# Forget sums of the attention added to the scores by a second product, and one expert matrix loaded at another place

## The reference, cut to what matters

```python
log_f = jax.nn.log_sigmoid(f_logit + b_forget)
cum = jnp.transpose(jnp.cumsum(log_f, axis=1), (0, 2, 1))
...
s = einsum('bqhd,bkhd->bhqk', qblk, kp) * scale
s = s + (cum[:, :, qs:qe, None] - cum[:, :, None, :qe])
s = jnp.where(s_pos <= t_pos, s, -inf)
p = softmax(s)
```

## Time and profile before

| what | value |
|---|---|
| time, median of three runs | 2497.79 us |
| the three runs | 2493.71, 2497.79, 2498.93 us |
| the profiled execution's own time | 2491.84 us |
| its span | 2490.1 us |
| PE busy | 1983.1 us, 80% |
| DVE, ACT, POOL busy | 1100.6, 421.6, 977.0 us |
| mean DMA rate over the span | 345 GB/s |

### The profile page before, as it was taken

One profiled execution on the slowest core, in us unless ns is written; L12 is line 12 of the kernel. 1 busy time (PEld: TensorE's weight loads), 2 busy tenths in 40 slices (PEclk: granted clock), 3 DMA queues, 4 the chain that ended last, 5 costly groups with the idle time before them and its releaser, 6 DMA issues.

```text
span 2490.1 us, 21117 instructions
## 1 busy us (share of the span) xinstructions
PE 1983.1 (80%) x7462; PEld 1022.2 (41%) x7462; DVE 1100.6 (44%) x2634; ACT 421.6 (17%) x1107; POOL 977.0 (39%) x1059
## 2 busy tenths in 40 slices
PE   8837997779988779989777777789999975566555
PEld 4523552235444225435322222248887732222221
DVE  6579638952457954455975444421012130000001
ACT  2312411201311111311111111101023110000000
POOL 0036757774556775546777777600000000000000
PEclk9868999999999999999999999999989988887887
DMA  6279999999999999999999999966543589999996
GB/s 221 93 262 338 409 402 407 409 409 399 402 357 406 409 409 402 399 372 342 409 409 409 409 409 409 410 208 166 151 101 121 191 342 426 428 426 427 427 427 266
DMA packets 228318, 860.19 MB, mean 345 GB/s; under 512 B 26080, under 2 KB 26592, under 8 KB 216432
## 3 DMA queue, kind: packets, MB, share of 16 engines
q0 software_dynamic: 147456, 536.94, 54.8%
q1 hardware_dynamic: 77488, 312.04, 33.1%
q10 hardware_dynamic: 3264, 9.80, 1.0%
HBM read 857.64 MB, written 1.05 MB: 345 GB/s over the span
## 4 chain that ended last, share of the span: by engine, by line
PE 37%; DMA 28%; DVE 18%; POOL 8%; issue 5%; ACT 2%; SPq 1%; DVEq 0%; ACTq 0%
PE psum L1840 13%; DMA rows<-in_peer_v,idx 8%; PE psum L2031 8%; DVE rows L1051 7%; PE psum L1832 6%; DMA rows<-in_w_e_gate 5%; POOL rows L691 4%; DMA rows<-in_w_e_down 4%; POOL rows L703 4%; DMA rows<-in_peer_u,idx 4%; DMA rows<-in_w_e_up 3%; PE psum L2234 3%; DMA rows<-in_gla_w_in 2%; PE psum L2257 1%; DVE work L934 1%
## 5 line engine op out<-in xcount | busy, mean ns | idle before, releaser
L2031 PE MATMUL psum<-rows,diag 128*128 128x512 f32 x2024 | 983.7, 625 | 264.6 <-ACT diag L1559 136.7
L1051 DVE CUSTOM_DVE_ANT_0 rows<-rows,psum 128x1024 f32<-128x1024 f32 x512 | 614.8, 1220 | 294.0 <-DMA rows<-in_peer_u,idx 283.2
L2031 PEld LDWEIGHTS psum<-rows,diag 128*128 128x128 f32 x2024 | 370.1, 195 | 832.1 <-issue 508.2
L691 POOL DMA_INDIRECT rows<-in_peer_u,idx x512 | 489.5, 956 | 378.2 <-DVEq L728 144.7
L703 POOL DMA_INDIRECT rows<-in_peer_v,idx x512 | 483.7, 945 | 272.6 <-PE psum L2031 148.6
L1840 PE MATMUL psum<-work,rows 128*128 128x256 f32 (+1 forms) x1664 | 287.9, 335 | 0.7 <-ACT work L1378 0.7
L1840 PEld LDWEIGHTS psum<-work,rows 128*128 128x128 f32 x1664 | 260.4, 193 | 31.0 <-issue 5.8
L1559 ACT ACTIVATE diag<-ident,wgt 128x128 f32<-128x128 f32 x506 | 166.0, 389 | 332.1 <-DVE wgt L1059 332.1
L2234 PE MATMUL psum<-rows,work 128*32 128x512 f32 x896 | 136.2, 693 | 106.0 <-DMA kept<-in_w_e_up 46.4
L1321 DVE TENSOR_TENSOR work<-kept,psum 128x512 f32<-128x512 f32 x8 | 8.2, 1030 | 423.2 <-PE psum L2234 423.2
L1378 ACT ACTIVATE work<-psum 128x512 f32<-128x512 f32 (+4 forms) x158 | 81.2, 532 | 547.7 <-PE psum L1840 194.9
(11 more groups left out here) (309 smaller groups left out, 1342.9 us busy)
## 6 DMA issues: line engine op xcount, KB each, us to landing
rows<-in_w_e_up SPq DMA_DIRECT2D x28, 2048.0 KB, 20.1
rows<-in_w_e_gate SPq DMA_DIRECT2D x25, 2048.0 KB, 20.5
rows<-in_w_e_down SPq DMA_DIRECT2D x24, 2048.0 KB, 20.9
rows<-in_w_in SPq DMA_DIRECT2D x32, 1024.0 KB, 9.6
rows<-in_gla_w_in SPq DMA_DIRECT2D x24, 1024.0 KB, 18.4
rows<-in_peer_w_query SPq DMA_DIRECT2D x16, 1024.0 KB, 9.2
rows<-in_peer_u,idx POOLq DMA_INDIRECT x512, 11.7
rows<-in_peer_v,idx POOLq DMA_INDIRECT x512, 12.1
```

The costliest lines, as they stand in the source:

```text
L691: pool.indirect_dma_start(out=u_rows[:, n % RU, :], out_offset=None, in_=a["peer_u"][g // 2], in_offset=bass.IndirectOffsetOnAxis(ap=idx[: ...
L1051: V_.tensor_tensor_reduce(out=u, in0=u, in1=tokens, scale=1.0, scalar=0.0, op0=ALU.mult, op1=ALU.add, accum_out=hid[:, r:r + 1]).then_inc( ...
L2031: last = mm(psum[:, 6 + c, :], diag[:, at % DIAGS, :], v_rows[:, n % RV, c * BANK:(c + 1) * BANK], start=r == 0, stop=summed(n + 1) == sum ...
```

## The change

The `fb` jobs, their copies, the bias tiles and DVE's two sums go. Each score product is left open and followed by a second one into the same columns of the bank, whose weight is the head's column of the identity repeated 128 times, and whose moving operand is the 16-row tile of running sums. So that they enter with the right sign, the scan subtracts. DVE adds the causal mask where it added the bias. PE waits for the copy of `k3` before the first scores. The first gate matrix (round 0, expert 0, place 0) is issued by ACT ahead of the mixer's first copy, once all value rows have been used.

```diff
-                + [f"fb{i}" for i in range(H // 2)]
...
-            return (["xn1", "abs", "cum", "convy", "bias"] + attention_order(0) + attention_order(1)[:4] + ["n0"]
+            return (["xn1", "abs", "cum", "convy"] + attention_order(0) + attention_order(1)[:4] + ["n0"]
...
-        x_bias = [carve(rows, 6144, H, P), carve(rows, 12288, H, S)]
...
-                    more = mask[:, 2 * P - w:].unsqueeze(1).to_broadcast([P, 2, w]) if bias is None else bias[:, h0:h1 + 1:2, :]
+                    more = mask[:, 2 * P - w:].unsqueeze(1).to_broadcast([P, 2, w])
...
-                link(V_.tensor_tensor_scan(x_cum[0:FH, 0:P], ones[0:FH, :], x_f[0:FH, 0:P], 0.0, ALU.mult, ALU.add))
+                link(V_.tensor_tensor_scan(x_cum[0:FH, 0:P], ones[0:FH, :], x_f[0:FH, 0:P], 0.0, ALU.mult, ALU.subtract))
                 link(V_.tensor_tensor_scan(x_cum[0:FH, P:S], ones[0:FH, :], x_f[0:FH, P:S], x_cum[0:FH, P - 1:P],
-                                           ALU.mult, ALU.add))
+                                           ALU.mult, ALU.subtract))
...
-                got(key, f"fb{H // 2 - 1}")
-                later = causal.unsqueeze(1).to_broadcast([P, H, P])
-                V_.tensor_tensor(x_bias[0], x_bias[1][:, :, 0:P], later, ALU.add)
-                link(V_.tensor_tensor(x_bias[1][:, :, P:S], x_bias[1][:, :, P:S], later, ALU.add))
-                V("bias", key)
-                attend(key, 0, x_S, 1.0, x_bias[0])
-                attend(key, 1, x_S, 1.0, x_bias[1], divide_0_behind=3)
+                attend(key, 0, x_S, 1.0)
+                attend(key, 1, x_S, 1.0, divide_0_behind=3)
...
                 act.wait_ge(v_taken, len(SHARED))
+                act.wait_ge(v_used, summed(NU))
+                load_matrix(act, 0, 0, 0, 0)
...
-                for i in range(H // 2):
-                    copy(key, f"fb{i}", x_bias[1][:, 2 * i:2 * i + 2, :])
...
-                load_matrix(act, 0, 0, 0, 0)
...
-                for i in range(H // 2):
-                    bank = open_bank(key, f"fb{i}")
-                    for e in range(2):
-
-                        pick = ident[0:FH, 2 * i + e:2 * i + e + 1].to_broadcast([FH, P])
-                        last = mm(bank[:, e * S:(e + 1) * S], pick, x_cum[0:FH, :], start=True, stop=True)
-                    close(key, f"fb{i}", last)
+                got(key, "k3")
...
-                            last = mm(banks[e], x_q[half, hh // 2, t * P:(t + 1) * P], x_k[half, hh // 2, 0:w], start=True, stop=True)
+                            mm(banks[e], x_q[half, hh // 2, t * P:(t + 1) * P], x_k[half, hh // 2, 0:w], start=True, stop=False)
+                            pick = ident[0:FH, hh:hh + 1].to_broadcast([FH, P])
+                            last = mm(banks[e], pick, x_cum[0:FH, 0:w], start=False, stop=True)
```

More of the change, by code:

```diff
@@ L778, in gain_piece, with attend @@
                 return piece_view(n)
-            def attend(key, t, Sb, scale, bias=None, divide_0_behind=None):
+            def attend(key, t, Sb, scale, divide_0_behind=None):
                 w = (t + 1) * P
@@ L791, in attend @@
                     bank = job_bank(key, f"S{t}_{g}")[:, 0:2 * w].rearrange("p (a w) -> p a w", a=2)
-                    h0, h1 = heads_of(g)
-                    more = mask[:, 2 * P - w:].unsqueeze(1).to_broadcast([P, 2, w]) if bias is None else bias[:, h0:h1 + 1:2, :]
+                    more = mask[:, 2 * P - w:].unsqueeze(1).to_broadcast([P, 2, w])
                     link(V_.scalar_tensor_tensor(s, bank, -scale, more, ALU.mult, ALU.add))
```

## The result

The changed kernel is slower: 2520.89 us (median of four, 2517.07 to 2523.61) against 2498.36, a ratio of 1.0088 with an interval of 1.0071 to 1.0106. That is +22.5 us where +8.1 was forecast, and outside the range. The profiled execution took 2517.07 us, with a span of 2515.3, 25.2 above. (In the kernel before, the table `BETWEEN` stands at L49 and `stage_jobs` at L75, not where the description above puts them.)

What follows compares the result with a forecast made beforehand. PE's chain of products through the mixer was taken to bound the kernel until the first `w_e_down` issue. Terms -10.84, +4.98, +3.56, +7.62 and -0.28 gave +5.0; one clock fall made +8.1, 2505.9 us, range 2493.5 to 2512.5.

Steps and rivals of the forecast that it cites:

- the release: End of the mixer: the first `w_e_down` loads, issued at 2029.73 us when gate products free places; DMA is full from then.
- the bias sums and copies: First attention block: eight ACT copies of 0.60 us and two DVE sums of 2.3 us go, worth nothing under `gc0`.
- the early load: First expert matrix, 2 MB, issued by ACT at about 1642.4 us: worth nothing, 0 taken for delay, bound 0.6 us.
- the price of a change: Score and pick products on PE: 0.13 us for each change of height, with bounds 0 and 0.2.
- the cost of the clock: Second attention block: one fall more to the lower clock expected, at 3.1 us, taking the sum from +5.0 to +8.1.
- leaving a score group: End of a score group on PE: about 0.2 us, from four records taking 1.06 us where streaming takes 0.88.
- the second pair: Opening pair of the second attention block: 4.63 us against 1.07, a loss of 3.56 us.
- the six second-block groups: Later score groups of the second attention block: 1.27 us added each, +7.62 us, less 0.28 for PE's wait.
- The first opening pair: First attention block, opening pair 2.87 us; with wait and `gc0` the stretch becomes 10.66 against 21.50, -10.84 us.
- changes are free: Rival for PE's score groups: going from 64 to 16 rows costs nothing; -1.5 us, 2496.3, chance 0.18.
- scores in the upper half run beside picks in the lower: Rival for the odd score groups: their scores cost nothing beside the picks; -8.1 us, 2489.7, chance 0.12.
- The case of two falls more: Rival for the attention blocks: the clock falls two times more; +11.2 us, 2509.0, at most +14.7, chance 0.12.

Runs made afterwards that it cites:

- `k128`: Changed kernel with picks over 128 rows, 112 of them zeros, in place of 16: 2504.09 us, ratio 1.0029 to the kernel before.
- `fb128`: Kernel before the change, with the picks of its `fb` jobs over 128 rows in place of 16: 2490.06 us against 2496.85, ratio 0.9976.
- `k64`: Changed kernel with picks over 64 rows, in the same half of the rows as the head's scores: 2494.25 us against 2497.21, ratio 0.9994.

## Why the prediction was wrong

The place was right: PE's chain through the mixer sets the release, DMA is empty before it, the bias sums and copies and the early load are worth nothing, and the sign was right, with the mechanism (changes of height, and the clock). The steps that failed are sizes: the price of a change and, far more, the cost of the clock.

1. **The price of a change.** I took 0.13 from the earlier trace rows; it is 0.19, near my upper bound of 0.2. The weights of the earlier trace rows have 64 columns, those here 128. `k128` has the heights of the earlier trace rows with 128-column weights, and it too pays 0.19, so the width fits and the heights don't matter. The kernel before had this price in sight: the 0.2 that I called leaving a score group is the same change, between products of 128 and 64 rows with 128-column weights. (It is paid on the way out as well: a quarter projection takes 6.91 us behind products of 128 rows, as in `k128`, and 7.10 behind products of 64 or 16. So the bare 256 columns are 0.43, and a change in the earlier trace rows is 0.14.) With all at the full clock, the sum by measured prices for the attention is -10.4 for the stretch to the end of `gc0` (0.73 + 3.3 + 7.1 = 11.1 against 21.50), +6.1, +3.9 for the second pair (5.0 as in `k128`), +8.6 for the six second-block groups: +8.2 where I had +5.0.
2. **The clock.** This was the large miss. The rest of the 24.0, 15.8 us by subtraction, is what the 1.2 GHz level cost beyond the kernel before, where I had 3.1: 3.4 at the first pair and `gc0`, 2.8 + 2.0 at the second pair and `ga3`, and 13.5 - 4 x 1.43 = 7.8 late in the second block (a little more in truth, since PE's waits shrank by 0.7 us there). I priced a fall by the one in the earlier trace rows, which had hit three short jobs and the start of a projection. That is no price for a fall: where the low products themselves go on, the lower clock goes on with them, and it nearly doubles them (1.15 for 0.62). I had the row that says so in hand, the `fb` jobs, where the clock stayed low as long as the 16-row products lasted and beyond. Late in the block I counted on nothing but what was there before; it fell at about 1931, at a PE that had no gap. Nor must every fall in the second block come from low products: `fb128` shows one at its opening without them.
3. **The first opening pair.** This is the first part of the second miss. I had 10.84 us as won there, which counts on the full clock through the pair and `gc0`. It fell again at the same place (3.83 us and 9.91 in place of 2.87 and 7.10), and 7.0 were won.

What the price of a change is made of can be read from the weight loads, PEld in the timeline; the first two lines are of the changed kernel, the next two of `k64`:

```profile
1839.41 0.29 PEld L2146 LDWEIGHTS psum<-diag,ident 16*128 16x128 f32 x2
1839.41 0.48 PE L2146 MATMUL psum<-diag,ident 16*128 16x128 f32 x2
...
1877.53 0.40 PEld L2149 LDWEIGHTS psum<-diag,ident 64*128 64x128 f32 x2
1877.74 0.59 PE L2149 MATMUL psum<-diag,ident 64*128 64x256 f32 x2
```

Where the height changes, the pick's weights begin to load together with the pick; where it stays, 0.21 us ahead of it, under the product before. One load takes 0.18 to 0.19 us for 128 columns, and 0.13 for the 64 of the earlier trace rows, close to the two prices. So the price may be a load that is no longer hidden. That fits these rows, but no run tested it.

The rivals: that changes are free failed, since every product beside a 16-row pick paid 0.19; picks of 64 rows in the score's half (`k64`) are cheap because nothing changes there. That scores in the upper half run beside picks in the lower failed too: an odd group takes as long as an even one. The case of two falls more, at most +14.7, was nearest; the clock was low in four stretches between 1818 and 1962 us in place of two, and they lasted longer than the one I had priced.

The Trainium skill, TensorEngine Tiling (Array Packing), Key Properties, says that a change of tiling mode drains the engine: the runs agree, 0.19 us a change with weights of 128 columns, and nothing where the mode stays (`k64`). The Trainium skill, TensorE: Matmul & The Clock Gate, What's actually happening, has the clock follow how busy PE is. Read as the profile's busy time, that isn't enough here: in the `fb` stretch the kernel before and `fb128` are both busy without a gap, and the clock fell in the one only.

Open: why the clock also fell at the first pair of `k128` and at the second block's opening in `fb128`, and what part pace and waits have beside rows.

## What to carry to other kernels

A small product put between others is not priced by its columns: look at whether its contraction has the height of its neighbours, and pad it with zero rows to that height if not. Rows of zeros cost no time on PE (a 256-column pick between scores took 0.63 us over 16 rows and over 128), and padding can win twice: by the change saved (`k64`) and by the clock kept (`fb128`: three lines, 6.8 us). Price a fall of the clock by the length of the work that goes on through it, not by another fall, and don't read its cause from one trace.

## What the runs showed of the hardware

- A change of height between products cost 0.19 us with 128-column weights, between 64 rows and 16 (the changed kernel) as between 64 and 128 (`k128`), and 0.14 with 64-column ones between 64 and 128. Adding into a bank and a repeated weight column cost nothing beyond the streaming (`k64`: 0.22 us for 128 columns).
- Sixteen products of 16 rows without a gap lowered PE's clock to 1.2 GHz (10.63 us); the same products over 128 rows (6.91), or over 64 in alternating halves (3.6), didn't. It also fell without low products, behind waits of PE (`k64` at 1924, `fb128` at 1879) and at the first pair of `k128`.
- Products in different halves of the rows and different banks ran at once (16 in 3.6 us in place of 6.9), by two products at most as far as two layouts show: blocks of four took 2.89 us, some 3.7 without overlap, and alternating pairs 2.03.
